# Experts' first layer in two f16 parts on a power of two, with the bound of the weights from a second reading

## The chip, the cores and the metric

One core of a Trainium2 chip runs the whole kernel. The metric is the device time of one execution in microseconds (us). Engines: PE (TensorE: matmuls, with its weight loads apart as PEld), DVE (VectorE), ACT (ScalarE), POOL (GpSimd) and SP, whose queue issues nearly all DMAs.

## The reference

Two transformer blocks run on 256 tokens of width 1024. The first mixes by a spatially gated unit, a forgetting attention and a cross attention to a memory, and has a feed-forward with a squared ReLU (1024 to 4096 and back). The second mixes by a state-space part and a convolution and ends in a layer of 16384 experts with 8 heads, each of which picks 16 by products of keys:

```python
def peer_ffn(x, w_query, sub_keys_1, sub_keys_2, w_down, w_up):
    q = (xt @ w_query).reshape(t, PEER_HEADS, PEER_DKEY)
    ...
    top_s, pos = lax.top_k(cand, PEER_TOPK)
    gate = jax.nn.softmax(top_s, axis=-1)
    ...
        u = w_down[ib]
        act = jax.nn.gelu(jnp.einsum("td,thkd->thk", xb, u), approximate=False) * gb
        v = w_up[ib]
        return jnp.einsum("thk,thkd->td", act, v)
```

x is the normalised residual. w_down and w_up are float32 of 16384 x 1024. All the kernel's matmuls with weights keep nearly float32 accuracy.

## The kernel before

**Weights as a stream.** All weights pass as 423 units of 128 x 1024 float32 (512 KB), in a fixed order (`STREAM`): w_in 0 to 16, memory 17 to 20, w_out 21 to 28, feed-forward 29 to 92, second block's input 93 to 132, its output 133 to 148, query 149 to 164, keys 165 to 166, experts down 167 to 294 (`U_DN`), experts up 295 to 422 (`U_UP`). SP's queue loads unit u into one of four buffers `raw` (`load_weights`, L293) as soon as the low part of unit u-4 is made. ACT rounds it to the high part (`hi_to`, L967) as soon as PE has finished unit u-3, since `W` has three slots. DVE subtracts to get the low part (`lo_to`, L1452). PE waits for the low part. Both parts are of the type fp32r. Each engine's program is one list written by hand: `hi_to` and `lo_to` stand in it between the other work, two units ahead of PE.

**Three products.** Activations are split the same way (XH, XL). `three` (L327 to L329) issues high x high, high x low and low x high into one bank. `h_unit` does so for the eight row tiles of a unit, 24 matmuls of 256 tokens, with the weights as the operand that is loaded. In the second block's input there are 272 tokens, in the experts' second layer 12 matmuls of 512 columns.

**Around the experts.** In the query stage (units 149 to 164) DVE makes the normalised activations T3 (`h_parts`) and their low parts XL, ACT their high parts XH. In the experts' first layer, unit c gives 128 experts' products for all tokens; ACT applies the GELU to every two units (L1417) and writes them to `hid`. DVE meanwhile runs the top-k search in c = 0 to 72, as a generator that is given a credit of 1.31 per unit and pays each operation's planned cost. From c = 77 to 127 it makes one-hot matrices (L2013 to L2021), which PE multiplies into gates (L894, 16 matmuls of f16 a step, 33 steps), and DVE multiplies the hidden values by them. At c = 127 ACT converts the first hidden tiles (`hidden_high(0)`), for which it waits for half of the last unit (`dn_half`), because HH lies in the space of XH.

**The other stages that the change touches.** The attention's 20 softmaxes (L1589 to L1593 on DVE, L1107 on ACT) run beside units 12 to 28; the low parts of the normalised memory (MNL, L1508) stand between them. The feed-forward is units 29 to 92. Units 117 to 132 go with short convolutions on DVE (L1739) fed by ACT's copies (L1238, L1245), beside long convolutions (L1707). L1873 is the last residual addition ahead of the query stage.

Of the kernel before, what the change touches and what calls it, by code (L numbers as in the profile page):

```python
# [51 lines left out]
T_TOPK, T_EXP, T_GATES, T_TAB, T_GATE = 72, 72, 73, 74, 77  # L52
TAIL = 32768 - 13056
# [3 lines left out]
SEMS = ("one_set d_x0 d_x1 d_v2 d_c1 d_cst d_vec d_mem d_sm d_out id16 mask "  # L57
        "hi lo unit sq ssum rs ri nt nh nl mt mn_h mn_l "
        "fg_mm fg_v fg_a np_mm np nr_mm nr tree qk_out fv_out gu_out mq_out km_out vm_out vn_v vn_a ws "
# [6 lines left out]
        "gs eb oa ob gm gh gl hh hl dn_half xt_in xt_out yb h3 fs d_nf fin").split()  # L66
# [27 lines left out]
def build(nc, io, out_d):  # L94
    ctx = ExitStack()
    with ctx:
# [26 lines left out]
        W = sb("W", [128, NSLOT, 2, 1024], F32R)  # L123
# [26 lines left out]

        LT, CM = (tensor(right, n, [128, 2176], F32, "right")[:, 0:1024].rearrange("p (s b) -> p s b", s=2)
# [73 lines left out]

        s = {n: ctx.enter_context(nc.semaphore(n)) for n in SEMS}
        d_raw = [ctx.enter_context(nc.semaphore(f"d_raw{i}")) for i in range(NRAW)]
# [26 lines left out]

        lf, lfa, lfx = small[:, 0:12], small[:, 12:24], small[:, 24:36]
# [7 lines left out]
        FS = small[:, 480:492]  # L263
        t3 = lambda a: a.rearrange("p (a b) -> p a b", b=16)
# [56 lines left out]
        def tensor_program(e):  # L321
# [47 lines left out]
            def first_pair(u, bank, i, xh, xl):  # L369
# [11 lines left out]
                for n in range(2):  # L381
# [5 lines left out]
                    t.then_inc(s["unit"], 1)  # L387

# [83 lines left out]
            def scores(n):  # L472
# [3 lines left out]
                if n == 0:  # L476
# [3 lines left out]
                    e.wait_ge(s["mask"], 1)  # L480
                    e.wait_ge(s["id16"], 1)
# [353 lines left out]
            for m in range(16):  # L835
                if m == 0:
                    first_pair(U_WQ, q_bank(0), 5, RH, RL)
                elif m > 1:
                    if m == 14:
                        e.wait_ge(s["nr"], 1)  # L840
# [4 lines left out]
                if m == 8:  # L845
                    e.wait_ge(s["ri"], N_NF)
                    for i in range(2):
                        t = e.transpose(ps[4][:, 256 + 128 * i:384 + 128 * i], RI[:, 0, 128 * i:128 * i + 128], ident)
                    t.then_inc(s["nr_mm"], 1)
# [49 lines left out]
            for c in range(128):  # L899
# [24 lines left out]
                h_unit(U_DN + c, ps[(c // 2) % 4][:, half(c)], C256, s["dn_half"] if c == 127 else None)  # L924
# [30 lines left out]
        def scalar_program(e):  # L955
# [5 lines left out]
            def hi_to(n):  # L961

                for u in range(made[0], min(n, NU)):
# [3 lines left out]
                    e.activation(W[:, u % NSLOT, 0, :], raw[:, u % NRAW, :], ACT.Copy).then_inc(s["hi"], 1)  # L967
                    made[0] = u + 1

# [382 lines left out]
            highs = h_high(2, T3, 256, U_WQ)  # L1352
            for m in range(16):
# [3 lines left out]
                if m > 5:  # L1357
                    next(highs, None)
# [875 lines left out]
```

## Time and profile before

| | |
|---|---|
| median of 3 runs | 1437.15 us (1435.28 to 1437.18) |
| span of the profiled execution (its own time) | 1438.5 us |
| PE busy | 1394.8 us, 97% |
| DVE busy | 1068.3 us, 74% |
| ACT busy | 734.9 us, 51% |
| mean granted clock of PE | 0.988 |

The profile gives the execution's span and no other time of it. Busy times of engines overlap. Matmuls are pipelined, so the length of one (280 ns) is not the distance to the next.

### The profile page before, as it was taken

How to read it: one execution, taken by the hardware profiler on the slowest of the kernel's cores; microseconds unless marked ns; L12 is line 12 of the kernel's file. 1: busy time of each engine (PE TensorE's matmuls, PEld its weight loads, DVE VectorE, ACT ScalarE, POOL GpSimd, SP SyncE). 2: the span in 40 equal slices, each digit the busy share in tenths (PEclk: the TensorE clock that was granted, in tenths of full speed). 3: DMA queues.
4: the chain of work that ended last, by engine and by line, in shares of the span. 5: the costliest groups of instructions: out<-in, count | busy, mean ns of one | idle time of the engine just before them, and what ended most of it. 6: DMA issues, size and time to landing. Idle time of an engine off the chain costs nothing.

```text
span 1438.5 us, 25239 instructions
## 1 busy us (share of the span) xinstructions
PE 1394.8 (97%) x10470; PEld 1281.2 (89%) x10470; DVE 1068.3 (74%) x1750; ACT 734.9 (51%) x1073; POOL 2.7 (0%) x9
## 2 busy tenths in 40 slices
PE   6999799998999999999999999999999999999997
PEld 6978799997999878999999999999987777888886
DVE  7654666545799998688999886888879888555554
ACT  6744655434556865676444445344443444444443
POOL 0000000000000000000000000000000000000000
PEclk9999899999999999999999999999999999999999
DMA  7423256564555201554655565555555555666653
GB/s 266 143 79 98 89 192 185 184 187 133 174 175 150 88 16 45 177 176 151 190 188 189 178 190 175 164 162 163 162 173 163 163 170 166 189 182 202 187 190 103
DMA packets 63618, 228.60 MB, mean 159 GB/s; under 512 B 7312, under 2 KB 8208, under 8 KB 63376
## 3 DMA queue, kind: packets, MB, share of 16 engines
q1 hardware_dynamic: 63072, 226.25, 50.6%
q8 instruction: 83, 1.36, 0.4%
q10 hardware_dynamic: 432, 0.74, 0.1%
q14 instruction: 31, 0.25, 0.1%
HBM read 225.91 MB, written 1.05 MB: 158 GB/s over the span
## 4 chain that ended last, share of the span: by engine, by line
PE 90%; DVE 7%; ACT 2%; issue 1%; DMA 0%; DVEq 0%; SPq 0%; ACTq 0%
PE ps L327 18%; PE ps L328 17%; PE ps L329 17%; PE ps L930 9%; PE ps L932 8%; PE ps L931 8%; PE ps L894 2%; PE ps L648 2%; DVE W L1452 1%; DVE RSI L1458 1%; PE ps L377 1%; DVE plain L1707 1%; PE ps L523 1%; PE ps L379 1%; ACT W L967 1%
## 5 line engine op out<-in xcount | busy, mean ns | idle before, releaser
L1452 DVE TENSOR_TENSOR W<-raw,W 128x1024 fp32r<-128x1024 f32 x423 | 517.1, 1226 | 278.8 <-ACT W L967 278.1
L967 ACT ACTIVATE W<-raw 128x1024 fp32r<-128x1024 f32 x423 | 446.2, 1057 | 401.6 <-PE ps L932 208.4
L327 PE MATMUL ps<-XH,W 128*128 128x256 f32 (+1 forms) x1552 | 442.7, 285 | 1.3 <-DVE hid L1904 0.7
L328 PE MATMUL ps<-XL,W 128*128 128x256 f32 (+1 forms) x1552 | 439.9, 283 | 0.0
L329 PE MATMUL ps<-XH,W 128*128 128x256 f32 (+1 forms) x1552 | 437.6, 282 | 0.0
L327 PEld LDWEIGHTS ps<-XH,W 128*128 128x128 f32 x1552 | 292.3, 188 | 2.9 <-issue 1.5
L329 PEld LDWEIGHTS ps<-XH,W 128*128 128x128 f32 x1552 | 294.2, 190 | 0.0
L328 PEld LDWEIGHTS ps<-XL,W 128*128 128x128 f32 x1552 | 292.9, 189 | 0.0
L930 PE MATMUL ps<-W,HH 128*128 128x512 f32 x512 | 205.6, 402 | 0.8 <-ACT hid L1417 0.8
L932 PE MATMUL ps<-W,HL 128*128 128x512 f32 x512 | 203.0, 396 | 0.0
L931 PE MATMUL ps<-W,HH 128*128 128x512 f32 x512 | 202.9, 396 | 0.0
L932 PEld LDWEIGHTS ps<-W,HL 128*128 128x128 f32 x512 | 96.4, 188 | 23.4
L930 PEld LDWEIGHTS ps<-W,HH 128*128 128x128 f32 x512 | 96.4, 188 | 23.0 <-issue 1.0
L931 PEld LDWEIGHTS ps<-W,HH 128*128 128x128 f32 x512 | 96.6, 189 | 22.0
L1417 ACT ACTIVATE hid<-ps 128x512 f32<-128x512 f32 x64 | 38.2, 598 | 114.9 <-PE ps L329 114.9
L328 PE MATMUL ps<-F1L,W 128*128 128x256 f32 x256 | 72.4, 283 | 0.0
L329 PE MATMUL ps<-F1H,W 128*128 128x256 f32 x256 | 72.4, 283 | 0.0
L327 PE MATMUL ps<-F1H,W 128*128 128x256 f32 x256 | 72.4, 283 | 0.0
L1707 DVE SCALAR_TENSOR_TENSOR plain<-plain,vec 128x256 f32<-128x256 f32 x156 | 66.1, 480 | 0.0
L2017 DVE TENSOR_TENSOR onehot<-RSI 128x1024 f16<-128x1024 f16 x64 | 44.2, 691 | 16.8 <-PE ps L894 15.7
L329 PEld LDWEIGHTS ps<-F1H,W 128*128 128x128 f32 x256 | 49.1, 192 | 0.0
L327 PEld LDWEIGHTS ps<-F1H,W 128*128 128x128 f32 x256 | 49.1, 192 | 0.0
(346 smaller groups left out, 1978.5 us busy)
## 6 DMA issues: line engine op xcount, KB each, us to landing
raw<-in_w_dn SPq DMA_DIRECT2D x128, 512.0 KB, 3.6
raw<-in_w_up SPq DMA_DIRECT2D x128, 512.0 KB, 3.9
raw<-in_w_ff SPq DMA_DIRECT2D x64, 512.0 KB, 4.1
raw<-in_w_in SPq DMA_DIRECT2D x57, 512.0 KB, 3.7
raw<-in_w_out SPq DMA_DIRECT2D x24, 512.0 KB, 3.5
raw<-in_w_q SPq DMA_DIRECT2D x16, 512.0 KB, 3.6
raw<-in_w_kv SPq DMA_DIRECT2D x4, 512.0 KB, 3.4
plain1a<-in_memT SPq DMA_DIRECT2D x1, 1024.0 KB, 10.7
```

Of the source, the lines that this page charges most:

```text
L327: e.matmul(out, wh, xh, start=first, stop=False, skip_group_check=shared)
L328: e.matmul(out, wh, xl, start=False, stop=False, skip_group_check=shared)
L329: return e.matmul(out, wl, xh, start=False, stop=last, skip_group_check=shared)
L648: e.matmul(ps[0 if j < 6 else 1][:, half(j)], DIAG[p % NDIAG], GP[:, j, 16 + k:272 + k], start=k == 0, stop=p + 1 == len(PE_TAPS) or PE_TA ...
L930: e.matmul(ps[b][:, :], HH[:, c % 8, tok], wh, start=c == 0, stop=False)
L931: e.matmul(ps[b][:, :], HH[:, c % 8, tok], wl, start=False, stop=False)
L932: return e.matmul(ps[b][:, :], HL[:, c % 8, tok], wh, start=False, stop=c == 127)
L967: e.activation(W[:, u % NSLOT, 0, :], raw[:, u % NRAW, :], ACT.Copy).then_inc(s["hi"], 1)
L1417: e.activation(hid_[:, 256 * c - 256:256 * c + 256], ps[(c // 2) % 4][:, :], ACT.Gelu).then_inc(s["gl"], 1)
L1452: e.tensor_tensor(W[:, u % NSLOT, 1, :], raw[:, u % NRAW, :], W[:, u % NSLOT, 0, :], ALU.subtract).then_inc(s["lo"], 1)
L1707: e.scalar_tensor_tensor(CV[:, j, :], GP[:, j, 16 + k:272 + k], V("ccw", 31 * j + k), CV[:, j, :], ALU.mult, ALU.add).then_inc(cv[j], 1)
L2017: e.tensor_tensor(OA, pairs(IOTA, 128), at(0, 128), ALU.is_equal).then_inc(s["oa"], 1)
```

## The change

The experts' first layer no longer uses fp32r parts. Its weights and activations are multiplied by powers of two and rounded to f16, and the rest, also multiplied, is rounded to f16 again. The GELU takes the product of the inverse scales. The scale of the activations comes from the norm's largest gain. That of the weights comes from the largest magnitude in w_down, which must be known before the layer starts: all 128 units of w_down are therefore loaded once more ahead of time, behind units 10 to 158 of the stream, into three buffers `PRE`, and DVE or ACT takes each one's maximum (DVE a true maximum of magnitudes; ACT the sum of magnitudes, an upper bound). Order and engine are written in `BOUND`: one per unit at 10 to 20, two (one on each engine) at 21 to 28, one at 29 to 91 with the engines in turn, two of three units at 103 to 132 on ACT, one at 141 to 158 in turn. `load_bounds` stands in SP's program right behind `load_weights`, and its wait is for the maximum three before.

```diff
+def _bound_order():
+    out = [(u, (PRE_V, PRE_A)[u % 2]) for u in range(10, 21)]
+    for u in range(21, 29):
+        out += [(u, PRE_V), (u, PRE_A)]
+    out += [(u, (PRE_V, PRE_A)[u % 2]) for u in range(29, 92)]
+    out += [(u, PRE_A) for u in range(103, 133) if u % 3]
+    out += [(u, (PRE_V, PRE_A)[u % 2]) for u in range(141, 159)]
...
+        def load_bounds(e, u):
+            for p in BOUND_AT.get(u, ()):
+                if u == BOUND[0][0]:
+                    e.wait_ge(s["one_set"], 1)
+                if p >= NPRE:
+                    by = BOUND[p - NPRE][1]
+                    e.wait_ge(s[by], bounds_made(p - NPRE + 1, by))
+                e.dma_start(PRE[:, p % NPRE, :], units[U_DN + p]).then_inc(d_pre[p % NPRE], 16)
...
                 load_weights(e, u)
+                load_bounds(e, u)
...
+            def dn_unit(u, out):
+                weights(u)
+                for k in range(8):
+                    t = three(out, slot16(u, slice(k * 128, k * 128 + 128)), (XH16[:, k, :], XL16[:, k, :]),
+                              k == 0, k == 7)
+                t.then_inc(s["unit"], 1)
...
                 if m == 8:
                     e.wait_ge(s["ri"], N_NF)
+                    e.wait_ge(s["scl"], 2)
+                    for n, top in enumerate((GMX, WMX)):
+                        e.transpose(ps[4][:, 128 * n:128 * n + 128], top.broadcast_to([128, 128]), ident)
...
-                h_unit(U_DN + c, ps[(c // 2) % 4][:, half(c)], C256, s["dn_half"] if c == 127 else None)
+                dn_unit(U_DN + c, ps[(c // 2) % 4][:, half(c)])
... (ScalarE, hi_to)
+                    if is16(u):
+                        if u == U_DN:
+                            e.wait_ge(s["scl"], 10)
+                        e.activation(W16[:, u % NSLOT, 0, :], raw[:, u % NRAW, :], ACT.Copy,
+                                     scale=S_W).then_inc(s["hi"], 1)
...
+                    for p in BOUND_AT.get(u, ()):
+                        if BOUND[p][1] == PRE_A:
+                            e.wait_ge(d_pre[p % NPRE], 16 * (p // NPRE + 1))
+                            e.activation(PRE[:, p % NPRE, :], PRE[:, p % NPRE, :], ACT.Abs,
+                                         accum_out=PMX[:, p:p + 1]).then_inc(s[PRE_A], 1)
...
-                if m > 5:
-                    next(highs, None)
+                if m == 11:
+                    e.wait_ge(s["scl"], 10)
+                if 11 <= m < 15:
+                    next(highs)
+                    next(highs)
...
-                    if k == 0:
-                        e.wait_ge(s["dn_half"], 1)
-                    else:
+                    if k:
...
-                                 ACT.Gelu).then_inc(s["gl"], 1)
+                                 ACT.Gelu, scale=S_OUT).then_inc(s["gl"], 1)
... (VectorE, lo_to)
+                    if is16(u):
+                        e.scalar_tensor_tensor(W16[:, u % NSLOT, 1, :], raw[:, u % NRAW, :], S_W,
+                                               W16[:, u % NSLOT, 0, :], ALU.mult, ALU.subtract).then_inc(s["lo"], 1)
...
+                    for p in BOUND_AT.get(u, ()):
+                        if BOUND[p][1] == PRE_V:
+                            e.wait_ge(d_pre[p % NPRE], 16 * (p // NPRE + 1))
+                            e.tensor_reduce(PMX[:, p:p + 1], PRE[:, p % NPRE, :], AX.X, ALU.max,
+                                            apply_absolute_value=True).then_inc(s[PRE_V], 1)
```

In the query stage DVE makes T3 one step earlier per unit (m = 5 to 12), takes the overall maximum at m = 7, makes the scales in `scales()` at m = 10 (ten operations on one or two columns, each waiting for the one before) and the low parts XL16 at m = 12 to 15. ACT makes the high parts XH16, two a unit, at m = 11 to 14. W16 lies in the space of W. XH16 and XL16 lie in the upper part of the space of HH and HL, so the first hidden tiles no longer wait for `dn_half`. Some semaphores are merged (`id16` into `mask`, `nr` into `np`, `fs` into `gs`), and the scratch space for dynamic DMAs is set to 1024.

## Rows read from the trace of the kernel before

**Rows 1.** The page: busy time of PE (part 1) and the chain (part 4).
```profile
PE 1394.8 (97%) x10470; PEld 1281.2 (89%) x10470; DVE 1068.3 (74%) x1750; ACT 734.9 (51%) x1073; POOL 2.7 (0%) x9
...
PE 90%; DVE 7%; ACT 2%; issue 1%; DMA 0%; DVEq 0%; SPq 0%; ACTq 0%
```

**Rows 2.** Windows: length, busy PE, PEld, DVE, ACT, POOL; clock, DMA share, GB/s.
```profile
167.00:347.00 180.00, 179.80 (x1504) 179.54 (x1503) 102.32 (x102) 89.05 (x106) 0.14 (x1) 1.00 0.60 185
...
430.00:480.00 50.00, 49.41 (x387) 48.20 (x387) 47.58 (x91) 32.84 (x61) 0.00 (x0) 1.00 0.52 158
...
668.00:806.00 138.00, 138.00 (x1164) 138.00 (x1163) 128.61 (x441) 65.23 (x78) 0.00 (x0) 1.00 0.59 183
806.00:872.00 66.00, 66.00 (x555) 65.89 (x555) 55.00 (x43) 29.93 (x35) 0.00 (x0) 1.00 0.58 184
...
885.00:1051.00 166.00, 166.00 (x1756) 164.50 (x1755) 132.22 (x181) 68.38 (x80) 0.00 (x0) 1.00 0.54 165
```

**Rows 3.** Timeline of PE in an experts' unit: start, length (us), instruction; 24 matmuls apart.
```profile
760.18 0.28 PE L327 MATMUL ps<-XH,W 128*128 128x256 f32 x1
...
763.03 0.28 PE L327 MATMUL ps<-XH,W 128*128 128x256 f32 x1
```

**Rows 4.** Timeline of PE at the state-space part, bf16.
```profile
513.72 0.38 PE L764 MATMUL ps<-MASK 128*128 128x512 bf16 x1 [0.66 <-DVE plain L1793]
513.94 0.61 PE L751 MATMUL ps<-plain 96*128 96x128 bf16 x8
514.38 0.44 PE L772 MATMUL ps<-plain 128*128 128x128 f32 x2
```

**Rows 5.** Groups by form, DVE: shapes, count, busy us, mean ns, idle before and releaser.
```profile
L1452 DVE TENSOR_TENSOR W<-raw,W 128x1024 fp32r<-128x1024 f32 x423 | 517.1, 1226 | 278.8 <-ACT W L967 278.1
...
L1580 DVE TENSOR_TENSOR MXL<-plain1a,MXH 128x256 fp32r<-128x256 f32 x8 | 3.4, 426 | 5.5 <-ACT MXH L1114 4.0 <-ACT MXH L1130 1.5
...
L1494 DVE SCALAR_TENSOR_TENSOR MXL<-X,vec,MXH 128x256 fp32r<-128x256 f32 x8 | 3.3, 481 | 5.6 <-ACT MXH L1012 5.6
...
L1555 DVE TENSOR_REDUCE small<-plain 128x12 f32<-128x768 f32 x1 | 1.0, 953 | 0.0
```

**Rows 6.** Groups by form, ACT.
```profile
L967 ACT ACTIVATE W<-raw 128x1024 fp32r<-128x1024 f32 x423 | 446.2, 1057 | 401.6 <-PE ps L932 208.4 <-PE ps L329 178.3 <-PE ps L385 5.9
...
L1107 ACT ACTIVATION_READ_ACCUMULATOR plain1a<-ps,small 128x1 f32 x20 | 3.9, 193 | 0.0
...
L997 ACT ACTIVATE RH<-X,vec 128x256 fp32r<-128x256 f32 x8 | 3.4, 495 | 0.1
...
L1001 ACT ACTIVATE MNH<-plain1a 128x256 fp32r<-128x256 f32 x8 | 2.8, 406 | 0.0
```

**Rows 7.** Timeline of DVE late in the top-k search.
```profile
827.37 1.23 DVE L1452 TENSOR_TENSOR W<-raw,W 128x1024 fp32r<-128x1024 f32 x1 [2.12 <-ACT W L967]
828.51 4.47 DVE L1975 TENSOR_REDUCE hid<-hid 128x128 f32<-128x2048 f32 x2
832.90 2.35 DVE L1452 TENSOR_TENSOR W<-raw,W 128x1024 fp32r<-128x1024 f32 x2
```

**Rows 8.** Window with full DMA queues, and the page's part 6 (median us to landing).
```profile
4.00:14.00 10.00, 4.50 (x21) 4.50 (x22) 6.77 (x11) 8.33 (x15) 0.00 (x0) 1.00 1.02 410
...
raw<-in_w_ff SPq DMA_DIRECT2D x64, 512.0 KB, 4.1
```

**Rows 9.** The chain that ended last at the attention's start: start, length, what.
```profile
66.41 0.95 ACT W L967
...
70.53 1.13 DVE W L1452
...
77.39 1.20 DVE MNL L1508 x2
78.96 0.56 ACT plain1a L1107 x2
```

**Rows 10.** Timeline of ACT: the absolute value right behind the square root of L1057.
```profile
55.94 0.20 ACT L1059 ACTIVATE small<-small 128x12 f32<-128x12 f32 x1
```

More of the change, by code:

```diff
@@ L52, with bounds_made @@
 T_TOPK, T_EXP, T_GATES, T_TAB, T_GATE = 72, 72, 73, 74, 77
+NPRE = 3
+PRE_A, PRE_V = "pm_a", "pm_v"
+def _bound_order():
[5 more added lines that the diff above has]
+    out += [(u, (PRE_V, PRE_A)[u % 2]) for u in range(141, 159)]
+    return out
+BOUND = _bound_order()
+assert len(BOUND) == 128
+BOUND_AT = {u: [p for p, (at, _) in enumerate(BOUND) if at == u] for u, _ in BOUND}
+def bounds_made(p, by):
+    return sum(1 for _, engine in BOUND[:p] if engine == by)
 TAIL = 32768 - 13056
 N_TK = 16 * 5 + 8 * 6 + 4 + 6
-SEMS = ("one_set d_x0 d_x1 d_v2 d_c1 d_cst d_vec d_mem d_sm d_out id16 mask "
+SEMS = ("one_set d_x0 d_x1 d_v2 d_c1 d_cst d_vec d_mem d_sm d_out mask "
         "hi lo unit sq ssum rs ri nt nh nl mt mn_h mn_l "
-        "fg_mm fg_v fg_a np_mm np nr_mm nr tree qk_out fv_out gu_out mq_out km_out vm_out vn_v vn_a ws "
+        "fg_mm fg_v fg_a np_mm np tree qk_out fv_out gu_out mq_out km_out vm_out vn_v vn_a ws "
         "sc mx ex rc pb tr pt av mixo mx_h mx_l sp_mm sp_v "
@@ L147, in build @@
         XL = tensor(right, "XL", [128, 8, 272], F32R, "right")
+        right.close()
+        right = stack()
+        XH16, XL16 = (tensor(right, n, [128, 4352], F16, "right")[:, 2304:4352].rearrange("p (a b) -> p a b", b=256)
+                      for n in ("XH16", "XL16"))
         right.close()
@@ L226, in build @@
         s = {n: ctx.enter_context(nc.semaphore(n)) for n in SEMS}
+        d_pre = [ctx.enter_context(nc.semaphore(f"d_pre{i}")) for i in range(NPRE)]
         d_raw = [ctx.enter_context(nc.semaphore(f"d_raw{i}")) for i in range(NRAW)]
@@ L263, in build @@
         FS = small[:, 480:492]
+        GMX, WMX, TOP2, FLR2, S_H, S_W, S_HW, S_OUT = (small[:, a:b] for a, b in (
+            (368, 369), (369, 370), (370, 372), (372, 374), (374, 375), (375, 376), (376, 377), (377, 378)))
         t3 = lambda a: a.rearrange("p (a b) -> p a b", b=16)
@@ L1351, in scalar_program, with scaled_high @@
                 square(SQ2[:, c:c + 2, 0:256], X[:, c:c + 2, :])
-            highs = h_high(2, T3, 256, U_WQ)
+            def scaled_high():
+                for c in range(8):
+                    e.wait_ge(s["nt"], 16 + c + 1)
+                    e.activation(XH16[:, c, :], T3[:, c, :], ACT.Copy, scale=S_H).then_inc(s["nh"], 1)
+                    yield
+            highs = scaled_high()
             for m in range(16):
@@ L1885, in vector_program @@
                     inverse(N_NF, 256)
-                if m > 4:
-                    next(parts, None)
-                if m == 10:
-                    e.wait_ge(s["nr_mm"], 1)
-                    e.tensor_copy(NR, ps[4][:, 256:512].rearrange("p (a b) -> p a b", b=128)[:, :, 0]).then_inc(s["nr"], 1)
+                if 4 < m < 13:
+                    e.scalar_tensor_tensor(T3[:, m - 5, :], X[:, m - 5, :], V("nffn", m - 5), RI[:, 0, 0:256],
+                                           ALU.mult, ALU.mult).then_inc(s["nt"], 1)
+                if m == 7:
+                    for by in (PRE_A, PRE_V):
+                        e.wait_ge(s[by], bounds_made(128, by))
+                    e.tensor_reduce(WMX, PMX[:, :], AX.X, ALU.max).then_inc(s["scl"], 1)
+                if m == 10:
+                    e.wait_ge(s["np_mm"], 2)
+                    e.tensor_copy(NR, ps[4][:, 256:512].rearrange("p (a b) -> p a b", b=128)[:, :, 0]).then_inc(s["np"], 1)
+                    scales()
+                if m > 11:
+                    c = 2 * (m - 12)
+                    e.wait_ge(s["nh"], 48 + c + 2)
+                    e.scalar_tensor_tensor(XL16[:, c:c + 2, :], T3[:, c:c + 2, :], S_H, XH16[:, c:c + 2, :], ALU.mult,
+                                           ALU.subtract).then_inc(s["nl"], 1)
                 if m % 2:
@@ L2222 @@
     }
-    nc = bacc.Bacc("TRN2", target_bir_lowering=False, num_devices=1)
+    nc = bacc.Bacc("TRN2", target_bir_lowering=False, num_devices=1, dynamic_dma_scratch_size=1024)
     io, feeds = {}, {}
```

56 lines of the change are left out of this document (42 added, 14 removed).

## The prediction

> **What bounds the kernel now.** I read the page first: PE is busy 97% of the span, and the chain that ends last is 90% PE [rows 1]. Then busy time by stage [rows 2]: in the feed-forward (167 to 347 us), the projections' last part (430 to 480) and the experts' first layer (668 to 1051) PE never rests, so a shorter matmul pays unit by unit as long as DVE and ACT can follow. DVE is the engine to watch: 47.6 of 50 us at 430 to 480 and 128.6 of 138 us beside the top-k search, against 132.2 of 166 us beside the gates.
>
> **1. The experts' matmuls (128 units of 24).** Eight groups of three take 763.03 - 760.18 = 2.85 us [rows 3], 118.8 ns a matmul of 256 columns. Before has no 256-column matmul in f16. The nearest rows are bf16: 512 columns start 0.22 us before the next matmul, and eight of 128 columns, each with its own weight load, take 0.44 us, or 55 ns each [rows 4]. Two of 128 make 110 ns; whatever is fixed in a matmul is then paid once and not twice, so I take 109.4 ns at 256 columns. Bounds: 118.8 (nothing gained) and 107.5 (half of 0.215, the least that a rounded 0.22 allows). At 109.4 a unit falls by 24 x 9.4 ns = 0.225 us to 2.62 us, and 128 units by 28.8 us. That is the ceiling.
>
> The Trainium skill (TensorE: Matmul & The Clock Gate, "Back-to-back issue gap") gives streams of weight load and matmul about 81 ns at 128 columns and 131 ns at 512. Halfway between these on its own scale is some 97 ns at 256, an estimate from that page, which would make the ceiling about 66 us. This case's rows show 55 ns and 0.22 us where the page has 81 and 131, and the measurement decides.
>
> **2. What DVE and ACT then allow.** The low part becomes a multiply-subtract with a scale per partition. With such a scale 256 columns take 481 ns, without it 426 [rows 5], so I take 1226 + 56 = 1282 ns (bounds 1226, and 1226 x 481/426 = 1384). The high part's scale adds 495 - 406 = 89 ns to 1057 [rows 6], hidden: ACT is busy under half of every stage of the layer [rows 2].
> - Beside the top-k search (668 to 806, 1164 matmuls, 48 units): PE alone would need 138 - 48 x 0.225 = 127.2 us. DVE has 128.6 + 48 x 0.056 = 131.3 us of work. DVE becomes the bound. I add 2 us of the start, where its work waits for transposes and banks: 133.5, a gain of 4.5 us. Top-k operations are issued by credits per unit, not by time, so they crowd each unit as it shortens.
> - 806 to 872 (23 units): DVE would hold 56.3 of 60.8 us, but its gathers are long. Two of them (4.47 us) stand between two low parts [rows 7]. From the conversion's start to the second low part's end it is about 1.15 + 1.28 + 4.4 + 1.28 = 8.1 us, and three units are 7.86. I take six such places (the search has 12 operations of this length in all, two at a time) at 0.25 us: gain 5.2 - 1.5 = 3.7 us.
> - 872 to 885: 6 units, 1.3 us.
> - Gates (885 to 1051, 1756 matmuls, of which 33 x 16 are gate products, so 51 units): PE 166 - 11.5 = 154.5 us, DVE 132.2 + 2.9 = 135.1. DVE keeps up, since the one-hots of a step need 1.8 us and it has 2.6: gain 11.5 us.
> Sum 21.0 us (bounds 0 and 28.8).
>
> **3. The second reading (128 loads of 512 KB, 128 maxima).** A VectorE maximum over 1024 elements: 953 ns for 768 [rows 5] plus 256 at 1.04 ns, about 1.2 us. On ScalarE: 1057 plus 193 ns for reading the accumulator [rows 6], less overlap, about 1.2 us.
> - *Feed-forward, units 29 to 91.* Each engine gets one per two units. DVE is busy 102.3 and ACT 89.1 of 180 us [rows 2]; 0.6 us per unit adds 38 us to each. Hidden, cost 0 (bounds 0 and 2). SP: the bound's load waits until the bound three before has been read, and behind it in SP's queue stands the next weight load. That wait ends about 1.2 us after the low part of unit u-3, while the conversion of u+1 starts three PE units after it: some 8 us for a landing of 4.1 us [rows 8]. Hidden while the engines of the DMA are not full, see rivals. If this cover fails, the conversion is late next, then PE.
> - *Attention's start.* The chain leaves PE here [rows 9]: conversion at 66.41, low part at 70.53, low parts of the memory at 77.39, exponential at 78.96. Unit 17's maximum stands on ACT before what follows the conversion, unit 18's on DVE before 77.39: together some 2.5 us (bounds 0 and 5, if all four maxima from 16 to 19 stand on it).
> - *Units 21 to 28, two each.* The second load waits for VectorE's maximum of the unit before, and ScalarE waits for its landing with the softmax's copies behind it. There is slack until the units come closer together at the end. I take 1 us (bounds 0 and 3).
> - *Units 103 to 132, two of three, on ScalarE.* 20 x 1.2 us = 24 us. ACT has room (32.8 of 50 us), but the outputs it copies feed DVE, which has 2.4 us of idle time in 50 [rows 2]. Some copies come 0.4 to 0.6 us late: 1.5 us (bounds 0 and 6).
> - *Units 141 to 158 and the scales.* Vector's maximum before the last residual addition (0 to 1.2 us), ten one-column operations (of 0.15 to 0.25 us) in the query stage where lows may lag by over a unit: 1 us (bounds 0 and 4).
> Removing the wait on half of the last unit, merging semaphores and the smaller scratch: 0. ScalarE then converts the first hidden tiles at or before its old time, and PE still waits for the last GELU. The GELU's scale adds 0.09 us there.
> Costs 2.5 + 1 + 1.5 + 1 = 6.0 us.
>
> **Sum.** 1438.5 - 21.0 + 6.0 = 1423.5 us of span. The page gives no total beside the span; the median of the runs lies 1.35 us under it. So 1422 us.
>
> **Rivals.**
> *The DMA becomes the bound (the other side).* The feed-forward's share is 0.60 at 185 GB/s [rows 2]. Twice the traffic would be a share of 1.20, and 180 us would become 216: 1422 + 36 = 1458 us. Against it: while many transfers are queued the same engines moved 410 GB/s over 10 us [rows 8], and two loads per unit are 2 x 0.524 MB in 2.87 us = 365 GB/s, so 89%. The share of scattered transfers holds waits that overlap in a full queue. It decides if the queued rate falls under 365 GB/s. Chance 0.10.
> The Trainium skill (DMA: Bandwidth & Descriptors, "Where 436 GB/s comes from") puts HBM at about 358 GB/s per core. By that page, an estimate, a unit needs 2.93 us, and 62 units cost 62 x 0.055 = 3.4 us, or 1425 us. The 410 GB/s of this trace is above that figure, if only for 10 us.
> *All is hidden.* DVE follows and the maxima cost nothing: 1437.15 - 28.8 = 1408 us, some 1410 with the start of the layer. For it: PE is dense at nearly all places of the added work. Against it: 131.3 us of DVE work at 668 to 806. Chance 0.10.
> *f16 is no faster at 256 columns*, the 118.8 ns being the stream's and not the type's: 1437 + 6 = 1443 us. Against it the bf16 rows. Chance 0.05.
> *Costs twice as large.* Maxima in front of softmax, convolutions and query projection add 12 us and the low parts stall PE: 1430 to 1440 us. Chance 0.10.
> *Absolute value calls for its own table.* 13 ScalarE maxima between exponentials and GELUs would cost 2 x 1.28 us each, 33 us, with perhaps half hidden: about 1439 us. ACT ran it behind a square root's table without a load of its own [rows 10]; behind the exponential's no row shows it. Chance 0.03.
> The Trainium skill (ScalarE: Activation LUTs, "Table sets: the hidden batching unit") says that absolute value is in every set, which would make this 0; no row here shows it for the exponential's.
>
> **Numbers.** The forecast, 1415 to 1430 us, has 0.62. Range: 1409 to 1438, which takes in "all is hidden" and most of "twice as large" and leaves the DMA, f16 and part of the table case out. About 0.2% (2.9 us) is what a measurement of this kernel can tell from no change. Faster: 0.62 + 0.10 + most of 0.10 = 0.79. Same: 0.05. Slower: DMA 0.10, f16 0.05 and a little = 0.16.
>
> **What would show it.** Eight groups of three in the experts take 2.62 us beside the gates; PE waits there for low parts under 1 us in all. At the top-k search DVE is busy over 97% and PE waits for the low part, units at 2.75 us or more. The low part takes 1.28 us. The feed-forward keeps its 180 us at near 365 GB/s. The step to 78.96 comes 2 to 3 us later. It is wrong if the feed-forward grows, if the gates' units stay at 2.85 us, or if table loads appear beside the maxima.

## The result, and the profile after

The changed kernel takes 1452.33 us (median of 4 runs, 1450.44 to 1453.7) against 1437.16 us (4 runs, 1435.28 to 1440.2) for the kernel before on the same chip: a ratio of 1.0112, 95% interval [1.009, 1.0134]. It is slower by 1.1%. The forecast was 1422 us, in a range of 1409 to 1438, so even the range missed. One kernel's executions differ here with the granted clock of PE: on one chip the kernel before took 1431.9 to 1433.4 us at a mean clock of 0.994 of full and 1439.7 to 1440.3 us at 0.987.

The page of the changed kernel has these lines (the busy time of part 1 and the chain that ended last by engine), to be set beside [rows 1].

```profile
span 1450.1 us, 25585 instructions
...
PE 1371.2 (95%) x10472; PEld 1215.6 (84%) x10472; DVE 1131.7 (78%) x1814; ACT 825.8 (57%) x1221; POOL 3.5 (0%) x9
...
PE 66%; DVE 22%; ACT 8%; issue 3%; DMA 1%; DVEq 0%; ACTq 0%; SPq 0%
```

PE's share of the last chain went from 90% to 66%, and DVE's from 7% to 22%. DVE is still busy only 78% of the span: it isn't full, and yet PE waits for it. The rows below say where.

**Where the time went.** The start of ScalarE's high part of unit u is a mark that both kernels share. The table gives its time in the changed kernel minus that in the kernel before (the offset), in us, both from the profiled execution, and the forecast of each stretch. The two spans, 1438.5 and 1450.1 us, differ by 11.7 us and the medians by 15.2: the span of 1438.5 us is that of executions which took 1440.3 us, 3 us over the median. Differences of 2 or 3 us between offsets can come from the clock alone; the last section has the rows.

| stretch (units) | offset at its start, at its end | change | forecast |
|---|---|---|---|
| first mixer's projections and attention (10 to 20) | -0.84, 2.24 | +3.1 | +2.5 |
| two maxima per unit (20 to 30) | 2.24, 4.01 | +1.8 | +1 |
| feed-forward (30 to 94) | 4.01, 30.64 | **+26.6** | 0 |
| second block up to unit 136 | 30.64, 30.12 | -0.5 | +1.5 |
| output projection, queries, scales (136 to 166) | 30.12, 31.77 | +1.7 | +1 |
| experts beside the search (166 to 218) | 31.77, 24.97 | -6.8 | -4.5 |
| experts, long gathers (218 to 240) | 24.97, 27.02 | **+2.1** | -3.7 |
| experts, gates (240 to 295) | 27.02, 12.21 | -14.8 | -12.8 with the 6 units ahead of them |
| second layer (295 to the end) | 12.21, 11.66 | -0.6 | 0 |

From unit 166 to the end the experts gave back 20.1 us where 21.0 were forecast. The four stretches of added work outside the feed-forward cost 6.0 us together, as forecast, though single ones were off in both directions. One stretch carries the error: the feed-forward, in which 63 maxima were costed at nothing.

**The experts** behave as forecast. This is the timeline of PE beside the gates (start, length, instruction): eight groups of three take 1002.64 - 1000.02 = 2.62 us, so 109.2 ns a matmul, against 2.85 us in [rows 3].

```profile
1000.02 0.27 PE L383 MATMUL ps<-XL,W 128*128 128x256 f16 x1
...
1002.64 0.27 PE L383 MATMUL ps<-XL,W 128*128 128x256 f16 x1
```

The groups by form give what the new and changed operations cost (columns: shapes, count, busy us, mean ns, idle before and its releaser); they answer to [rows 5] and [rows 6].

```profile
L1537 DVE SCALAR_TENSOR_TENSOR W<-raw,small,W 128x1024 f16<-128x1024 f32 x128 | 162.8, 1276 | 31.6 <-ACT W L1035 31.6
...
L1546 DVE TENSOR_REDUCE PMX<-PRE 128x1 f32<-128x1024 f32 x54 | 65.5, 1212 | 0.0
...
L1035 ACT ACTIVATE W<-raw,small 128x1024 f16<-128x1024 f32 x128 | 146.3, 1143 | 78.1 <-PE ps L384 78.1
L1043 ACT ACTIVATE PRE<-PRE 128x1024 f32<-128x1024 f32 x74 | 77.4, 1045 | 8.2 <-DMA PRE<-in_w_dn 8.2
...
L1043 ACT ACTIVATION_READ_ACCUMULATOR PRE<-PRE 128x1 f32 x74 | 13.8, 187 | 0.0
```

The low part takes 1276 ns (1282 forecast), the high part 86 ns more than the plain one (89), VectorE's maximum 1212 ns and ScalarE's 1045 and 187 ns with a small overlap (about 1.2 us each). Every price was right. No table load stands at L1043, and the loads that there are match those of the kernel before one for one: absolute value called for none between exponentials and GELUs. The Trainium skill (ScalarE: Activation LUTs, "Table sets: the hidden batching unit") says that abs is in every set; by that rule, the trace agrees.

**The feed-forward** does not. These are two windows of the changed kernel (length, busy time of PE, PEld, DVE, ACT and POOL, then clock, DMA share and GB/s). The first lies beside units 38 to 61, in the first of the two feed-forward layers, the second beside the other layer.

```profile
190.00:280.00 90.00, 73.85 (x598) 71.39 (x596) 58.60 (x63) 53.08 (x76) 0.00 (x0) 1.00 0.82 291
...
290.00:370.00 80.00, 80.00 (x657) 80.00 (x656) 51.08 (x45) 47.39 (x65) 0.00 (x0) 0.98 0.97 356
```

In the first PE rests 16 of 90 us, although DVE has 31 us to spare, ACT 37 and the DMA 18% of its time. In the second the same 0.5 maxima per engine and unit and the same transfers cost nothing. So neither the volume of work nor the traffic explains the loss. What differs is the work around them. In the first layer VectorE makes the ReLU of each pair of units (L1742) and ScalarE squares it (L1231) and rounds it (L1233). The timelines of ACT and DVE over one pair, with the idle time before each instruction and its releaser in brackets:

```profile
249.48 1.04 ACT L1038 ACTIVATE W<-raw 128x1024 fp32r<-128x1024 f32 x1
250.43 1.04 ACT L1043 ACTIVATE PRE<-PRE 128x1024 f32<-128x1024 f32 x1
...
251.47 1.04 ACT L1038 ACTIVATE W<-raw 128x1024 fp32r<-128x1024 f32 x1
255.53 0.63 ACT L1231 ACTIVATE plain<-plain 128x512 f32<-128x512 f32 x1 [3.02 <-DVE plain L1742]
256.20 0.63 ACT L1233 ACTIVATE F1H<-plain 128x512 fp32r<-128x512 f32 x1
256.73 1.04 ACT L1038 ACTIVATE W<-raw 128x1024 fp32r<-128x1024 f32 x1
```
```profile
250.56 1.23 DVE L1540 TENSOR_TENSOR W<-raw,W 128x1024 fp32r<-128x1024 f32 x1 [1.72 <-ACT W L1038]
252.54 1.22 DVE L1540 TENSOR_TENSOR W<-raw,W 128x1024 fp32r<-128x1024 f32 x1 [0.76 <-ACT W L1038]
253.69 1.21 DVE L1546 TENSOR_REDUCE PMX<-PRE 128x1 f32<-128x1024 f32 x1
254.82 0.68 DVE L1742 SCALAR_TENSOR_TENSOR plain<-ps,RSI 128x512 f32<-128x512 f32 x1
```

Read by start times this is a closed ring: ScalarE's high part 249.48, its maximum 250.43, the next high part 251.47, VectorE's low part of it 252.54, its maximum 253.69, the ReLU 254.82, the square 255.53, the rounding 256.20, and again the high part at 256.73. That is 7.25 us for two units, where the matmuls need 5.71. Each engine executes its own program in order and waits on the other: ACT once per turn (3.02 us), DVE twice (1.72 and 0.76). The two maxima stand in the ring with 1.04 and 1.13 us; without them these starts add up to 5.08 us. The kernel before shows a turn without maxima, at a place where PE holds nothing up:

```profile
188.09 2.10 ACT L967 ACTIVATE W<-raw 128x1024 fp32r<-128x1024 f32 x2
192.16 0.63 ACT L1155 ACTIVATE plain<-plain 128x512 f32<-128x512 f32 x1 [1.97 <-DVE plain L1649]
192.83 0.63 ACT L1157 ACTIVATE F1H<-plain 128x512 fp32r<-128x512 f32 x1
193.37 1.04 ACT L967 ACTIVATE W<-raw 128x1024 fp32r<-128x1024 f32 x1
```
```profile
189.17 2.36 DVE L1452 TENSOR_TENSOR W<-raw,W 128x1024 fp32r<-128x1024 f32 x2 [1.72 <-ACT W L967]
191.44 0.68 DVE L1649 SCALAR_TENSOR_TENSOR plain<-ps,RSI 128x512 f32<-128x512 f32 x1
```

From high part to high part it is 193.37 - 188.09 = 5.28 us, through both low parts on DVE. That fits into 5.71 us with 0.43 to spare. (5.28 and the two maxima are more than 7.25: the first low part now runs beside ACT's maximum.) In the changed kernel the squares follow each other at 7.25 us fourteen times in a row. Sixteen pairs at 7.25 - 5.71 = 1.54 us would be 24.6 of the 26.6 us. At units 40, 46, 52 and 58 the offset is 11.60, 16.23, 20.85 and 25.48: three such steps between each two of them. From unit 64 on it stands still.

### The profile page after: what moved, and what is told of

Same layout as the page of the kernel before. It is cut to its first block, busy times and chain, and to the rows that moved or that the text cites. A ratio compares the mean times of both kernels' runs of the same rounds, so it can differ in the third digit from the quotient of the medians.

```text
span 1450.1 us, 25585 instructions
## 1 busy us (share of the span) xinstructions
PE 1371.2 (95%) x10472; PEld 1215.6 (84%) x10472; DVE 1131.7 (78%) x1814; ACT 825.8 (57%) x1221; POOL 3.5 (0%) x9
## 4 chain that ended last, share of the span: by engine, by line
PE 66%; DVE 22%; ACT 8%; issue 3%; DMA 1%; DVEq 0%; ACTq 0%; SPq 0%
PE ps L382 11%; PE ps L384 10%; PE ps L383 10%; PE ps L995 8%; PE ps L997 8%; PE ps L996 8%; DVE W L1537 5%; ACT W L1038 3%; DVE W L1540 2%; PE ps L959 2%; DVE PMX L1546 2%; PE ps L710 2%; ACT PRE L1043 1%; DVE RSI L1551 1%; DVE hid L2046 1%
## 5 line engine op out<-in xcount | busy, mean ns | idle before, releaser
L1540 DVE TENSOR_TENSOR W<-raw,W 128x1024 fp32r<-128x1024 f32 x295 | 360.3, 1223 | 214.3 <-ACT W L1038 214.2
L1038 ACT ACTIVATE W<-raw 128x1024 fp32r<-128x1024 f32 x295 | 310.9, 1056 | 268.9 <-PE ps L997 208.4
L382 PE MATMUL ps<-XH,W 128*128 128x256 f16 (+2 forms) x1552 | 432.7, 279 | 27.0 <-DVE W L1540 17.1
L383 PE MATMUL ps<-XL,W 128*128 128x256 f16 (+2 forms) x1552 | 430.5, 277 | 0.0
L384 PE MATMUL ps<-XH,W 128*128 128x256 f16 (+2 forms) x1552 | 430.4, 277 | 0.0
L382 PEld LDWEIGHTS ps<-XH,W 128*128 128x128 f16 (+1 forms) x1552 | 200.2, 129 | 47.1 <-issue 23.9
L384 PEld LDWEIGHTS ps<-XH,W 128*128 128x128 f16 (+1 forms) x1552 | 200.5, 129 | 12.0
L383 PEld LDWEIGHTS ps<-XL,W 128*128 128x128 f16 (+1 forms) x1552 | 200.4, 129 | 11.2
L1035 ACT ACTIVATE W<-raw,small 128x1024 f16<-128x1024 f32 x128 | 146.3, 1143 | 78.1 <-PE ps L384 78.1
L1537 DVE SCALAR_TENSOR_TENSOR W<-raw,small,W 128x1024 f16<-128x1024 f32 x128 | 162.8, 1276 | 31.6 <-ACT W L1035 31.6
L1501 ACT ACTIVATE hid<-ps,small 128x512 f32<-128x512 f32 x64 | 44.0, 688 | 96.0 <-PE ps L384 95.9
L1043 ACT ACTIVATE PRE<-PRE 128x1024 f32<-128x1024 f32 x74 | 77.4, 1045 | 8.2 <-DMA PRE<-in_w_dn 8.2
```

What stands on the lines that cost most here:

```text
L382: e.matmul(out, wh, xh, start=first, stop=False, skip_group_check=shared)
L383: e.matmul(out, wh, xl, start=False, stop=False, skip_group_check=shared)
L384: return e.matmul(out, wl, xh, start=False, stop=last, skip_group_check=shared)
L1035: e.activation(W16[:, u % NSLOT, 0, :], raw[:, u % NRAW, :], ACT.Copy, scale=S_W).then_inc(s["hi"], 1)
L1043: e.activation(PRE[:, p % NPRE, :], PRE[:, p % NPRE, :], ACT.Abs, accum_out=PMX[:, p:p + 1]).then_inc(s[PRE_A], 1)
L1537: e.scalar_tensor_tensor(W16[:, u % NSLOT, 1, :], raw[:, u % NRAW, :], S_W, W16[:, u % NSLOT, 0, :], ALU.mult, ALU.subtract).then_inc(s["l ...
```

## The experiments

Each ratio is against the kernel before on the same chip, with its 95% interval. Offsets are those of the table above, in each kernel's own trace.

**Without a second reading (e1_no_second).** What the f16 layer is worth alone.

```diff
 def _bound_order():
...
-    return out
+    return []
...
-    e.tensor_reduce(WMX, PMX[:, :], AX.X, ALU.max)
+    e.tensor_scalar(WMX, cst[:, C_ONES:C_ONES + 1], 32.0, None, ALU.mult)
```

> The changed kernel without any second reading: no loads, no maxima, the bound of the weights is a constant of 32. What is left is the f16 layer. Theory: the 20 us from the first to the last unit of the experts' first layer stay, the costs ahead of it (25.6 us in the feed-forward, 4.6 us before it, some 1.5 us in the query stage) go: 1437 - 20 = 1417 us, at most 1419 us. If the f16 layer gains less without the late start, 1420 us or more.

Measured: 1414.99 us (1414.36 to 1416.96), ratio 0.9853 [0.9819, 0.9887]. From unit 170 to the end the offset falls from -5.46 to -25.42, by 20.0 us: the forecast of the layer stands. Another 5.5 us came before the experts: 3.0 by unit 16 and 2.8 between units 22 and 24. At 105 to 122 us, windows of the kernel before (first) and of this one show why the second part is not to be counted on:

```profile
105.00:122.00 17.00, 16.42 (x84) 12.03 (x83) 7.51 (x19) 7.58 (x21) 0.00 (x0) 0.80 0.21 63
```
```profile
105.00:122.00 17.00, 16.25 (x111) 13.02 (x110) 9.16 (x21) 7.89 (x21) 0.00 (x0) 1.00 0.23 74
```

The mean granted clock was 0.80 there in the kernel before (and in the changed kernel) and 1.00 here. PE's clock has two levels, 1.2 and 2.4 GHz, so both earlier kernels ran some 40% of these 17 us at the lower one.

**Transfers alone, and maxima alone (e2_loads_only, e3_maxima_only).** In units 31 to 62, 32 units beside the first feed-forward layer, one half of the second reading is taken out at a time. In e2 the maxima of those units are left out, and each transfer waits only for the landing of the one three before. In e3 their transfers are left out and the maxima are taken of what the buffer holds, each behind the maximum three before.

```diff
 # e2
-    if BOUND[p][1] == PRE_V:
+    if BOUND[p][1] == PRE_V and not QUIET(u):     # the same for PRE_A; QUIET: 31 <= u < 63
 # e3, load_bounds
     for p in BOUND_AT.get(u, ()):
+        if QUIET(u):
+            continue
```

> The changed kernel with the second loads of units 31 to 62 kept and their maxima left out (the scale comes from the other units' maxima). Theory, order: in the feed-forward's first layer the conversion, the low part, the ReLU, the square and the high part of the result form one ring through ScalarE and VectorE, and both maxima stand in it; without them units 34 to 64 take 5.71 us per pair again instead of 7.25, and the median falls by 25 us to about 1427 us. Rival, transfers: twice the traffic sets the pace there; then it stays at 1452 us.

> The changed kernel with the second loads of units 31 to 62 left out and their maxima kept, on what lies in the buffers. Theory, order: the pair of units still takes 7.25 us, the median stays at about 1452 us. Rival, transfers: pairs back at 5.71 us, about 1427 us.

Measured: e2 1425.54 us (1422.09 to 1428.18), ratio 0.9923 [0.9896, 0.9949]; e3 1452.77 us (1449.02 to 1455.55), ratio 1.011 [1.007, 1.0149]. The windows over the stretch, e2 first:

```profile
180.00:280.00 100.00, 100.00 (x842) 100.00 (x841) 67.06 (x71) 59.12 (x76) 0.00 (x0) 1.00 0.98 363
```
```profile
190.00:280.00 90.00, 74.23 (x603) 71.99 (x602) 59.30 (x63) 51.92 (x75) 0.00 (x0) 1.00 0.47 145
```

With all the traffic (363 GB/s) and no maxima in the first layer PE never rests. With the maxima and no traffic it rests as in the changed kernel (74.23 of 90 us, against 73.85). The maxima's places in the programs cost the time, and the transfers' volume doesn't.

**The maxima in other places (e4_order).** The odd units' maximum goes to VectorE and is handed out behind the ReLU and the low part of the hidden tiles; the even units' goes to ScalarE, behind the high part, while VectorE makes the low part and the ReLU.

```diff
-    out += [(u, (PRE_V, PRE_A)[u % 2]) for u in range(29, 92)]
+    out += [(u, (PRE_A, PRE_V)[u % 2]) for u in range(29, 92)]
...
     if BOUND[p][1] == PRE_V:
+        if 31 <= u < 63:
+            late.append(p)
+        else:
+            largest(p)
...
     if m % 2 and m > 1:
         f_relu(m // 2 - 1)
+    if m % 2:
+        while late:
+            largest(late.pop(0))
```

> The changed kernel with the same loads and maxima, two of them in other places: for units 29 to 91 the engines change turns, so that ScalarE's maximum comes behind the second conversion of a pair (where it waits for the ReLU), and for units 31 to 62 VectorE's comes behind the ReLU and the low part of the result. Theory, order: the ring is back at 5.1 us, PE at 5.71 us per pair, the median at about 1427 us, faster than before the change by some 10 us. Rival, transfers: no change, 1452 us. Rival, sum of busy times (each engine simply has too much work): no change either.

Measured: 1440.57 us (1435.35 to 1443.71), ratio 1.003 [1.0012, 1.0048]. The expectation missed: 12 us came back and not 25. The list of waits between 180 and 280 us (total, times, longest, in us) names something new:

```profile
DVE W L1547 <- ACT W L1038: 24.1, 26, 2.6
ACT PRE L1043 <- DMA PRE<-in_w_dn: 19.1, 15, 3.0
ACT W L1038 <- DMA raw<-in_w_ff: 11.3, 13, 2.0
```

In the changed kernel no wait for a DMA is in the list of this stretch. Three experiments ask what it is.

**Where the second loss sits (e8_order_noload, e7_shift, e14_half_bytes).** e8 is e4 without the transfers of units 31 to 62 (maxima of what the buffer holds). e7 is e4 with each bound's transfer two units further back in SyncE's program, so that it can't hold up the weights' transfers. e14 is e4 with half the columns in each such transfer, so the other half stays out of the bound.

```diff
 # e7, sync_program
     load_weights(e, u)
-    load_bounds(e, u)
+    load_bounds(e, u - 2)          # for the bounds of units 31 to 62
 # e14, load_bounds, units 31 to 62
-    e.dma_start(PRE[:, p % NPRE, :], units[U_DN + p])
+    e.dma_start(PRE[:, p % NPRE, 0:512], units[U_DN + p][:, 0:512])
```

> The order of e4_order with the second reading's transfers of units 31 to 62 left out: the maxima there are taken of what PRE holds, so part of the weights' bound is not computed from the weights. Both landing theories (SyncE's order, and busy DMA engines) expect 1427 us (1422 to 1430), since nothing then stands in SyncE's queue and nothing competes. Rival, the ring between VectorE and ScalarE is still too long with the maxima reordered: 1438 us or more, as in e4_order (1440.6).

> The exchanged and deferred maxima of before (e4_order), and in SyncE's program the second reading's transfer of each of units 31 to 62 stands two units later, behind the first reading's transfer of unit u+2 instead of unit u. Theory now, the third in-order program (SyncE's): in e4_order the second reading's transfer waited for a deferred maximum and held the first reading's next transfer behind it, so raw landed late (18 us of ScalarE's waits for PRE and 11 us for raw between 180 and 270 us). With the order changed those waits are gone, the feed-forward units go back to the matmuls' 5.71 us per pair, and the time is 1427 us (1423 to 1431), against 1440.6 of e4_order. Rival, the DMA engines are too busy to land both readings in time: 1438 us or more, with the share over 0.9 in 170 to 270 us.

> The order of e4_order, with the second reading's transfer of each of units 31 to 62 cut to half its columns (0 to 511, so the other half of those units doesn't enter the bound); waits, buffers and maxima are untouched. e4_order kept 14 us over the same order without transfers. Theory now, the DMA engines have next to no room there: 1,049 KB per 2.855 us are 367 GB/s, and the highest rate that a run showed over such a stretch is 378 GB/s, so that each pause in issuing is lost for good. With half the bytes (275 GB/s) pauses are made up: 1427 us (1424 to 1431). Rival, the waits on the three buffers and the landing's fixed part, not its volume: 1437 us or more, as in e4_order (1440.6).

| kernel | median us (range) | ratio to before | offset at unit 64 |
|---|---|---|---|
| changed | 1452.33 (1450.44 to 1453.7) | 1.0112 [1.009, 1.0134] | 30.72 |
| e4 | 1440.57 (1435.35 to 1443.71) | 1.003 [1.0012, 1.0048] | 22.30 |
| e7 | 1442.34 (1441.38 to 1444.04) | 1.005 [1.003, 1.007] | 19.99 |
| e14 | 1431.47 (1428.02 to 1438.27) | 0.9974 [0.9955, 0.9994] | 11.50 |
| e8 | 1426.34 (1425.36 to 1426.95) | 0.9936 [0.9917, 0.9954] | 5.98 |

The windows of e4, e7, e14 and e8, in this order (in e14 and e8 they reach 18 to 23 us into the second layer, where the transfers are whole again):

```profile
180.00:280.00 100.00, 90.58 (x717) 88.45 (x717) 72.17 (x77) 65.33 (x92) 0.00 (x0) 0.97 0.87 317
```
```profile
180.00:280.00 100.00, 88.58 (x705) 86.63 (x704) 72.90 (x78) 65.39 (x94) 0.00 (x0) 0.97 0.85 306
```
```profile
180.00:280.00 100.00, 94.68 (x785) 93.51 (x784) 79.31 (x83) 70.95 (x98) 0.00 (x0) 1.00 0.81 273
```
```profile
180.00:280.00 100.00, 99.65 (x837) 99.45 (x837) 81.61 (x85) 73.05 (x101) 0.00 (x0) 1.00 0.66 218
```

e8 shows that the new order opens the ring of the two engines: PE is busy 99.65 of 100 us with every maximum in place. So the rest of e4's loss needs the transfers. e7 was expected at 1427 us and refutes what I thought of them: with SyncE's program out of the way the waits for raw are gone, but those for PRE grow to 33 us in the same stretch, and the time stays. The sign of its rival, DMA engines over 0.9 busy, isn't there either (0.85). e14 takes half the bytes of each and gets 10.8 of the 16.3 us at unit 64 back. Two transfers of 524 KB per 2.855 us are 367 GB/s. e2 shows that the DMA engines do it when they are always fed (0.98 busy, 363 GB/s). In e4 a bound's transfer waits until the maximum three before has freed its buffer, the engines pause (0.87 busy, 317 GB/s), and little room is left to catch up: the highest rate in a row of this text is 394 GB/s (last section). With 275 GB/s to deliver most of the pauses are made up. A part of the 10.8 us is clock: it was 0.97 in e4's and e7's windows and 1.00 in the others, which costs e4 at most some 3 us (an estimate: 6 of 100 us at half speed). The effect of the bytes remains without it. At a mean clock of 0.989 e4's executions took 1435.35 and 1439.05 us, and e14's, at 0.988 and 0.989, 1428.02 to 1429.06 us. My expectation for e14 was 1424 to 1431 us and it came at 1431.47; 5.5 us at unit 64 stay unexplained by volume. In e14 ACT's waits for PRE fell from 19.1 to 10.0 us and those for raw stayed (10.2 against 11.3), so when the transfers start, in SyncE's program and behind three buffers, still counts. A kernel with more buffers would tell more, and wasn't tried.

**SyncE's order alone (e9_shift_only).** The changed kernel with nothing but e7's shift.

> The changed kernel, with nothing but SyncE's order changed as in e7_shift; the maxima stand where the change put them. Theory, the ring between VectorE and ScalarE alone sets 7.25 us per pair there, with the weights landed in time: 1452 us as the changed kernel, within 2 us. Rival, SyncE's order is already part of the changed kernel's loss: 1440 to 1448 us.

Measured: 1454.62 us (1453.62 to 1455.23), ratio 1.0132 [1.0113, 1.0151]. It gains nothing (the intervals of the two overlap). In the changed kernel the ring sets the pace, and SyncE's order adds nothing that shows.

**The searches' operations one at a time (e10_single_ops).** Beside the search VectorE's operations were taken from both searches at once, two by two, before the credit was looked at again.

```diff
-    for t in list(best):
-        cost = next(t, None)
-        if cost is None:
-            best.remove(t)
-        else:
-            credit -= cost
+    t = best.pop(0)
+    cost = next(t, None)
+    if cost is not None:
+        credit -= cost
+        best.append(t)
```

> The changed kernel, with VectorE's operations of the two top-k searches handed out one at a time, in turn, with the credit looked at after each, instead of two at a time. Theory, the lumps: two 2.28 us operations in a row between low parts are what keeps TensorE waiting (3.2 us at 838, 1.1 at 861) in units 218 to 240, where my forecast missed by 5.7 us: gain of 3 to 5 us, 1448 us (1446 to 1450). Rival, VectorE is full there (1.28 us low part and 1.31 us of search per unit against 2.62 us of matmuls), so only the volume counts: 1451 to 1453 us.

Measured: 1446.94 us (1446.57 to 1447.77), ratio 1.0081 [1.0063, 1.0099]: 5.4 us less than the changed kernel. The timelines of DVE at the same work, the changed kernel first:

```profile
834.61 1.28 DVE L1537 SCALAR_TENSOR_TENSOR W<-raw,small,W 128x1024 f16<-128x1024 f32 x1
835.80 4.49 DVE L2089 TENSOR_TENSOR hid<-hid,cst 128x2048 f32<-128x2048 f32 x2
840.21 3.67 DVE L1537 SCALAR_TENSOR_TENSOR W<-raw,small,W 128x1024 f16<-128x1024 f32 x3
843.79 4.48 DVE L2096 TENSOR_TENSOR hid<-hid 128x2048 f32<-128x2048 f32 x2
```
```profile
838.92 2.48 DVE L1537 SCALAR_TENSOR_TENSOR W<-raw,small,W 128x1024 f16<-128x1024 f32 x2
841.31 2.29 DVE L2089 TENSOR_TENSOR hid<-hid,cst 128x2048 f32<-128x2048 f32 x1
843.51 1.28 DVE L1537 SCALAR_TENSOR_TENSOR W<-raw,small,W 128x1024 f16<-128x1024 f32 x1
844.70 2.29 DVE L2096 TENSOR_TENSOR hid<-hid 128x2048 f32<-128x2048 f32 x1
```

In the changed kernel PE's next matmul starts 3.17 us after that of 838.46, with the pair of gathers of 835.80 in front of three low parts, and again 1.13 us after that of 861.52 (they are 0.11 us apart when nothing is waited for). With single operations the longest such distance of this stretch is 0.96 us. From unit 218 to unit 240 the offset now falls by 4.2 us (25.88 to 21.68), where the changed kernel's rose by 2.1. The forecast for it was a fall of 3.7.

**Placed otherwise, everything computed (e12_thin_single, e13_attn, e15_last).** In e12 only the even ones of units 31 to 62 carry a bound, on ScalarE; the 16 others go to ScalarE at 16 places in units 93 to 138, and e10's edit is in. In e13 the maxima of units 16 to 19 move to units 129, 132, 144 and 146 as well. In e15 the last two of these stand at units 92 and 100.

```diff
-    out += [(u, (PRE_V, PRE_A)[u % 2]) for u in range(29, 92)]
+    out += [(u, (PRE_A, PRE_V)[u % 2]) for u in range(29, 92) if u % 2 == 0 or not 31 <= u < 63]
+    out += [(u, PRE_A) for u in (93, 94, 97, 98, 102, 105, 108, 111, 114, 117, 120, 123, 126, 133, 137, 138)]
```

> The whole second reading, placed otherwise: of units 31 to 62 only the even ones carry a bound, on ScalarE, behind the high part during which VectorE makes the low part and the ReLU; the other 16 go to ScalarE at units 93, 94, 97, 98, 102, 105, 108, 111, 114, 117, 120, 123, 126, 133, 137 and 138; and the searches' operations are handed out one at a time as in e10_single_ops. If order and DMA room in the first feed-forward layer are the cause, its 25.6 us go, the searches give 5.4 (e10), and the 16 moved maxima cost 0 to 3 us: 1423 us (1420 to 1427). Rival, the moved maxima cost their full 1.24 us each where ScalarE is busy: 1438 us. Rival, even 16 maxima lengthen the ring: over 1432 us.

> As e12_thin_single, and the maxima of units 16 to 19 are moved too, to ScalarE at units 129, 132, 144 and 146. In the changed kernel units 16 to 20 lose 3.6 us that the kernel without a second reading does not lose. Theory, ScalarE's and VectorE's chain through the attention's start has no room for a maximum of 1.2 us: 3 to 4 us less than e12_thin_single (about 1420 us). Rival, the place is covered by other waits: as e12_thin_single within 1 us.

> As e13_attn, with the two maxima that stood at units 144 and 146 at units 92 and 100 instead, on ScalarE too. In e13_attn the start of unit 150 against the kernel before was 2.7 us later than that of unit 142's stretch allowed (1.84 us at unit 136, 4.58 at unit 150), while the maxima at 129 and 132 cost nothing. Theory, units 144 and 146 already carry a second reading at 394 GB/s, so a second one there isn't landed in time: without them 2 to 3 us less than e13_attn, 1417.3 us (1415 to 1420). Rival, ScalarE is what is late wherever the two stand: 1419 to 1421 us.

| kernel | median us (range) | ratio to before | offset at units 20, 64, 136, 150, end |
|---|---|---|---|
| e12 | 1420.38 (1417.44 to 1423.31) | 0.9901 [0.9877, 0.9925] | 2.36, 2.56, 3.04, 3.09, -21.58 |
| e13 | 1420.07 (1419.52 to 1421.28) | 0.9898 [0.9878, 0.9918] | -1.54, 0.89, 1.84, 4.58, -20.32 |
| e15 | 1417.05 (1416.56 to 1417.59) | 0.987 [0.985, 0.989] | -2.19, 0.38, 1.13, 1.18, -23.44 |

The window of e12, for the first feed-forward layer:

```profile
190.00:280.00 90.00, 90.00 (x758) 90.00 (x757) 60.12 (x64) 66.40 (x92) 0.00 (x0) 1.00 0.86 301
```

PE doesn't rest any more, while ACT is busier than in the changed kernel (66.40 against 53.08 us) and DVE no less (60.12 against 58.60): more work in the same time, in an order that closes no ring over 5.71 us. e12's time lies in its expected range. From unit 64 to unit 150, over the sixteen moved maxima, its offset rises by 0.5 us where the changed kernel's falls by 0.6, so they cost about 1.1 us together. e13 missed its expectation: it leads e12 by 3.9 us at unit 20, but by 1.7 at unit 64, gives 2.7 back at units 136 to 150, and takes as long as e12 in the end. A part of its lead at unit 20 is clock (last section). e15 puts the two maxima of units 144 and 146 elsewhere, and its time is 3.0 us less than e13's, as expected. Its expectation gave late landing as the reason for the 2.7 us. The list of waits of e13 beside these units (586 to 611 us) has:

```profile
ACT W L1040 <- DMA raw<-in_w_out: 3.9, 2, 2.5
DVE PMX L1548 <- DMA PRE<-in_w_dn: 2.4, 2, 1.5
ACT PRE L1045 <- DMA PRE<-in_w_dn: 2.3, 4, 1.5
```

With another 1.4 us for raw these are 10 us of waits for transfers, where e15's list of the same window has 0.3 us and e12's none. So the landing is late there. The DMA engines are only 0.86 busy at 332 GB/s in this window, where e15's are 0.95 busy at 364 GB/s. So their rate alone isn't the limit; what starts the transfers late was not tried. e15 is 1.3% faster than the kernel before and 35 us faster than the changed one, with the whole second reading in it.

## Why the prediction was wrong

- **f16 pace, the ceiling.** Right: 109.2 ns where 109.4 was taken. The 97 ns that the prediction works out from the Trainium skill's figures (TensorE: Matmul & The Clock Gate, "Back-to-back issue gap") isn't halfway: on a straight line 256 columns lie a third of the way from 81 ns to 131 ns, at 97.7 ns, an estimate from that page, and the ceiling by it is 65 us. Its sum doesn't use it, and the measured 109.2 ns decides.
- **What DVE and ACT allow.** Right in sum, 20.1 us against 21.0 (20.0 in e1). Two terms were off against each other. Beside the search the gain was 6.8 and not 4.5 us. In units 218 to 240 it was -2.1 and not 3.7: I had put each place with two gathers at 0.25 us, and the rows show 3.17 and 1.13 us for two of them. The prediction named the lumps and priced them as if their delays didn't add up in an engine with next to no idle time; e10 shows that they are the cause.
- **Attention's start.** 2.5 us forecast, 3.1 us read from the offset from unit 10 to 20. The four maxima from 16 to 19 cost 3.6 us in most kernels and 2.1 us in e2 and e7, where the clock stayed up (last section); both lie within the bounds.
- **Units 103 to 132.** Forecast 1.5 us, measured none. The eight further maxima of e12 there cost about 0.5 us.
- **Feed-forward, units 29 to 91: "Hidden, cost 0 (bounds 0 and 2)".** This is the step that failed, by 26.6 us, and with it the sign. I compared busy time with room (102.3 and 89.1 of 180 us [rows 2]) and found 38 us more on each engine well covered. The average is right and says nothing here. The two in-order programs wait for one another once per pair of units. What counts is the sum along the closed path through both. The kernel before takes 5.28 us where PE doesn't hold it up, so 0.43 us of slack per pair of 5.71 us, and 2.2 us were put in. The profile of before had the evidence: in each pair ACT waits for DVE's ReLU and DVE for ACT's high part. The prediction's own sign of being wrong, a feed-forward that grows, is what came. My first check of the cover went through SP's queue and the landing, and not through this path. Where the path doesn't exist, in the second layer, the cost was the forecast zero.
- **From span to median.** The prediction took the median as 1.35 us under the span. These belong to different executions: each time of the result lies 1.8 to 1.9 us above its own span. It did no harm, since 1437.15 - 21.0 + 6.0 is 1422 us as well.
- **Rivals.** The DMA as the bound gave 1458 us, nearest to the result, and is refuted as its cause: e3 is as slow without the transfers, e2 fast with them. Nor is the rate without weight here: once the ring is opened, asking for 367 GB/s leaves so little room that pauses cost time (e4, e14). The Trainium skill's figure of about 358 GB/s, weighed in the prediction (DMA: Bandwidth & Descriptors, "Where 436 GB/s comes from"), stands against e2's 363 GB/s over 100 us, at which PE had no wait; the measurement decides. The table rival and "f16 is no faster" are refuted by the rows above. "All is hidden" and "costs twice as large" fail by the 6.0 us that the stretches outside the feed-forward cost.

## What to carry to other kernels

Before work is added to an engine with idle time, follow the waits from it to the other engine and back until the path closes, and add up the starts along it: the slack is the period less that sum, and not the idle share. Where the trace has a turn in which nothing else holds the path up, read the sum there. Put added work where its engine would wait for the other one anyway, and in single pieces where the engine is nearly full; the same maxima cost 26 us in one place and about 1 us in others. When a first limit is removed, look at once for the next one, here a DMA rate with little room for pauses, and test it by size (half the bytes) as well as by order.

## What the hardware showed beyond expectation

The DMA engines of this core carried 394 GB/s over 20 us while PE kept its pace (changed kernel, 620 to 640 us):

```profile
620.00:640.00 20.00, 19.88 (x166) 19.68 (x165) 15.04 (x16) 12.20 (x19) 0.00 (x0) 1.00 1.00 394
```

The Trainium skill (Perfetto Trace Analysis, "Roofline") says that a core that is alone on its memory domain can draw about a fifth more than the 358 GB/s of its share; by that page, this row agrees. The granted clock differs between executions of the same work, and with it a few us. From 105 to 122 us it was 0.80 in the kernel before, in the changed one, in e3, e4 and e10, and 1.00 in e1, e2 and e8: between units 22 and 24 e2 and e8 gain 2.0 us on the kernel before and e1 2.8, which no edit was aimed at. From 81 to 87 us it was 0.72 in the changed kernel, e3, e4, e8, e10 and e12, and 1.00 in e2 and e7, with the same work: there units 16 to 20 cost 3.6 us, and 2.1 us in the latter two. PE's rest around it was alike: it was busy 27.60 of the 32 us from 60 to 92 us in the changed kernel and 27.70 in e2. e13, without these four maxima, had 1.00 and a cost of 0.1 us. What decides which level is granted was not tried.
